# A second mixer's projections, norms, rotations and loads in another order

## The reference, cut to what matters

```python
hn = rms_norm(h, g_mix)
c_q, c_kv, k_r, q_d, k_d, v_d = split(hn @ w_in)      # 384, 256, 32, 512, 512, 512 columns
q  = rms_norm(c_q, g_cq) @ w_uq                       # 8 heads of 64 plain + 32 rotated features
kv = rms_norm(c_kv, g_ckv) @ w_ukv                    # 8 heads of 64 key + 64 value features
q_rope, k_rope = apply_rope(q[..., 64:]), apply_rope(k_r)        # k_rope is shared by the heads
o_mla = softmax((q_nope . k_nope + q_rope . k_rope) * scale) @ v_m
qd, kd = apply_rope(q_d), apply_rope(k_d)             # first 16 of 64 features of 8 heads
o_dil = dilated_attention(qd, kd, v_d)                # three masked patterns merged, as one mask
h = h + concat(rms_norm(o_mla), rms_norm(o_dil)) @ w_out
h = h + peer_ffn(...)                                 # product-key memory, then a gated embedding
```

## Time and profile before

| | |
|---|---|
| median of three runs | 2959.86 us (2959.3 to 2966.66) |
| profiled execution | 2961.28 us, span 2959.5 us, mean granted clock 0.967 |
| busy over the span | PE 2708.4 us (92%), DVE 1463.9 (49%), ACT 510.1 (17%), POOL 720.5 (24%) |
| second projection (to the end of its products) | 1341 to 1472 us |
| latent expansion | 1472 to 1544.7 us |
| attention's first scores | 1544.7 us |

### The profile page before, as it was taken

The page is one execution under the profiler, slowest core; times in us unless marked ns, Lnnn a source line. Parts: engine busy times, 40 slices in busy tenths (PEclk is TensorE's granted clock), DMA queues, the critical chain, the costliest instruction groups (busy, mean ns, idle before and its releaser), DMA issues. The chain is left out here.

```text
span 2959.5 us, 27511 instructions
## 1 busy us (share of the span) xinstructions
PE 2708.4 (92%) x10046; PEld 1524.1 (51%) x10046; DVE 1463.9 (49%) x3202; ACT 510.1 (17%) x1131; POOL 720.5 (24%) x588
## 2 busy tenths in 40 slices
PE   6999999999999689979989996999989889998888
PEld 3445634446444333324435565888879743333333
DVE  1045401203012322232137579889799986777773
ACT  2033300011001111221127420111122200000004
POOL 0000000000000011100000016655566565655640
PEclk9999999999999699999989998999999999999999
DMA  5101161210122899951210229999999699999983
GB/s 218 57 29 56 61 268 65 96 57 15 60 82 90 342 418 388 394 230 69 92 43 1 95 72 324 409 400 409 417 370 412 236 367 397 413 413 413 412 356 121
DMA packets 137559, 678.53 MB, mean 229 GB/s; under 512 B 20050, under 2 KB 21458, under 8 KB 105554
## 3 DMA queue, kind: packets, MB, share of 16 engines
q1 hardware_dynamic: 55986, 396.76, 33.5%
q0 software_dynamic: 80640, 276.88, 24.1%
q10 hardware_dynamic: 800, 3.15, 0.3%
HBM read 697.68 MB, written 33.55 MB: 247 GB/s over the span
## 5 line engine op out<-in xcount | busy, mean ns | idle before, releaser
L513 PE MATMUL ps<-hT,pm_coef_table 128*128 128x256 f32 (+1 forms) x2432 | 507.1, 371 | 30.4 <-DVE hT L439 24.4
L513 PEld LDWEIGHTS ps<-hT,pm_coef_table 128*128 128x128 f32 x2432 | 444.3, 192 | 87.2 <-issue 25.1
L2566 PE MATMUL ps<-hT 128*128 128x512 f32 x896 | 398.3, 598 | 41.6 <-DMA hT<-in_peer_v 28.2
L513 PE MATMUL ps<-hT,wring 128*128 128x512 f32 (+2 forms) x976 | 411.9, 583 | 10.5 <-PEq L694 2.9
L2415 POOL DMA_INDIRECT wring<-in_peer_u,pm_rows x256 | 336.0, 1313 | 300.8 <-DVE pm_coef L2676 159.3
L2415 POOL DMA_INDIRECT wring<-in_peer_v,pm_rows x256 | 325.0, 1269 | 235.0 <-DVE h_tok L2843 193.9
L2843 DVE SCALAR_TENSOR_TENSOR h_tok<-wring,pm_coef,h_tok 128x1024 f32<-128x1024 f32 x256 | 324.0, 1281 | 106.6 <-DMA wring<-in_peer_v,pm_rows 105.9
L2676 DVE CUSTOM_DVE_ANT_0 wring<-wring,pm_coef_table 128x1024 f32<-128x1024 f32 x256 | 303.2, 1218 | 35.0 <-DMA wring<-in_peer_u,pm_rows 34.4
L2566 PEld LDWEIGHTS ps<-hT 128*128 128x128 f32 x896 | 165.4, 190 | 274.3 <-issue 189.7
L513 PEld LDWEIGHTS ps<-hT,wring 128*128 128x128 f32 (+1 forms) x976 | 185.0, 191 | 231.6 <-issue 229.7
L1634 POOL DMA_INDIRECT hT<-xn_dram_out,row_token x24 | 24.5, 1020 | 1148.9 <-issue 1004.1
(11 more groups left out here) (423 smaller groups left out, 2829.5 us busy)
## 6 DMA issues: line engine op xcount, KB each, us to landing
ex_gu<-in_experts SPq DMA_DIRECT2D x32, 2048.0 KB, 19.3
pm_coef_table<-in_peer_uT SPq DMA_DIRECT2D x64, 1024.0 KB, 8.0
hT<-in_peer_v SPq DMA_DIRECT2D x64, 1024.0 KB, 8.0
ex_dn<-in_experts SPq DMA_DIRECT2D x47, 1024.0 KB
wring<-in_w_in SPq DMA_DIRECT2D x21, 2048.0 KB, 7.8
wring<-in_experts SPq DMA_DIRECT2D x15, 2048.0 KB
ada_w<-in_w_ada SPq DMA_DIRECT2D x12, 2048.0 KB, 12.1
g_dram_out<-pm_coef_table SPq DMA_DIRECT2D x56, 256.0 KB, 9.4
```

Of the source, the lines that this page charges most:

```text
L513: mm = env.nc.tensor.matmul(out, w[:, k, lo:hi], rhs(k), start=(k == 0), stop=(k == KD - 1))
L2566: mm = nc.tensor.matmul(env.ps[:, OUT[k], :], scores_at(i)[:, k // 2 * P:(k // 2 + 1) * P], vr[p % 2][:, i % 2 * D + k % 2 * WBLK:i % 2 * ...
```

## The change

1. In the projection the latents and the shared key part come before the values, with the list of weight blocks in the new order (0, 1, 3, 4, 2).
2. The squares, roots, inverses and scalings of the latents move from the expansion into the projection: on ScalarE behind the copy of the shared key part and ahead of the values' copies, on VectorE behind the rotation.
3. The four loads of the expansion are issued in the projection, ahead of the ring's loads. Their buffers are allocated around both stages.
4. In the expansion the transposed latents are copied out by VectorE (tiles 0, 2, 4) and ScalarE (tiles 1, 3). TensorE rotates the shared part first and waits only for the three query tiles before the queries' products and for the two others before the keys'. The heads' rotations stand ahead of the keys' products.
5. VectorE awaits the mask in front of the first step of kind 1.

```diff
@@ stage_second_project
-    blks = [env.take_block(t) for t in (q_t[-1], k_t[-1], v_t[-1], c_t[-1], kr_t)]
+    blks = [env.take_block(t) for t in (q_t[-1], k_t[-1], c_t[-1], kr_t, v_t[-1])]
 ...
             @block.sync
                 nc.sync.dma_start(perm[:], dram["perm_dil"]).then_inc(tab_in, 16)
+                nc.sync.dma_start(M.wq[:], dram["w_uq"]).then_inc(M.tab_in, 16)
+                nc.sync.dma_start(M.wkv[:], dram["w_ukv"]).then_inc(M.tab_in, 16)
+                nc.sync.dma_start(M.tab[0:QH], dram["rope_mla"]).then_inc(M.tab_in, 16)
+                nc.sync.dma_start(M.perm[0:QH, 0:QH], dram["perm_mla"]).then_inc(M.tab_in, 16)
                 load_blocks(env, sp)
 ...
             @block.scalar
                 nc.scalar.activation(M.kr[:], env.ps[0:QH, kr_t[0], :], ACT.Copy).then_inc(env.bank_free[kr_t[0]], 1)
+                for t in c_t + e_t:
+                    evacuated(env, act, t)
                 n = 0
                 for p, (lo, w) in enumerate(parts):
 ...
+                for i, t in enumerate(v_t):
+                    product_done(env, act, t)
+                    nc.scalar.activation(M.dv[:, i, :], env.ps[:, t[0], :], ACT.Copy).then_inc(env.bank_free[t[0]], 1)
 ...
             @block.vector
                 rope_dve(env, v, r_t, lambda j: M.dqk[:, j, :], tab, sn, cos_s, rope_s)
+                v.wait_ge(rms_s, 2)
+                nc.vector.reciprocal(ss[:], rs[:]).then_inc(inv_s, 1)
 ...
@@ stage_latent_expand
             @block.tensor
-                to_features(env, pe, c_t, lambda t, j: M.c[:, t, j * P:(j + 1) * P],
-                            lambda t, j: pe.wait_ge(nrm_s, (t + 1) + (NT if j >= CQ else 0)))
+                to_features(env, pe, c_t, lambda t, j: M.c[:, t, j * P:(j + 1) * P], lambda t, j: None)
                 pe.wait_ge(tab_in, 64)
-                for t in c_t:
+                rope_mm(env, pe, r_t[:1], perm[0:QH, 0:QH], roped, lambda j: None)
+                for t in c_t[:CQ]:
                     evacuated(env, pe, t)
 ...
+                rope_mm(env, pe, r_t[1:], perm[0:QH, 0:QH], lambda j: roped(j + 1), lambda j: evacuated(env, pe, q_t[j]))
+                for t in c_t[CQ:]:
+                    evacuated(env, pe, t)
 ...
-                rope_mm(env, pe, r_t, perm[0:QH, 0:QH], lambda j: M.q[:, j, :] if j < AH else M.kr[:],
-                        lambda j: evacuated(env, pe, q_t[j]) if j < AH else None)
@@ stage_attention
-                v.wait_ge(mask_in, 16)
                 for s in range(ns + 3):
                     if s < ns:
                         kind, hp, qt = steps[s]
+                        if kind == 1 and sem_of(s) == 0:
+                            v.wait_ge(mask_in, 16)
@@ program
-        stream(env, "w_in2", "w_out2", "w_ple_gate")
+        for b in (0, 1, 3, 4, 2):
+            env.blocks.append(dram["w_in2"][b])
+        stream(env, "w_out2", "w_ple_gate")
```

More of the change, by code:

```diff
@@ L1930, in stage_second_project @@
     q_t, k_t, r_t = env.tiles(4), env.tiles(4), env.tiles(8)
-    v_t, c_t = env.tiles(NT), env.tiles(NT)
+    c_t = env.tiles(NT)
     e_t, kr_t = env.tiles(NT), env.tile()
-    blks = [env.take_block(t) for t in (q_t[-1], k_t[-1], v_t[-1], c_t[-1], kr_t)]
+    v_t = env.tiles(NT)
+    blks = [env.take_block(t) for t in (q_t[-1], k_t[-1], c_t[-1], kr_t, v_t[-1])]
     tab_in, cos_s, rope_s = (env.sem("sp_" + n) for n in ("tab", "cos", "rope"))
+    sq_s, rms_s, inv_s, nrm_s = (env.sem("le_" + n) for n in ("sq", "rms", "inv", "nrm"))
+    parts = ((0, QR), (QR, KVR))
     with ExitStack() as st:
@@ L1951, in _ @@
                                          scale=DH ** -0.5 if j < 4 else 1.0).then_inc(env.bank_free[t[0]], 1)
[L1952 to L1955, removed]
+                for i, t in enumerate(c_t):
+                    product_done(env, act, t)
+                    nc.scalar.activation(M.c[:, i, 0:WBLK], env.ps[:, t[0], :], ACT.Copy).then_inc(env.bank_free[t[0]], 1)
                 for i, t in enumerate(e_t):
@@ L1985, in stage_latent_expand @@
[L1985 to L2012, removed]
@@ L2023, in _ @@
                     nc.scalar.activation(rs[:, p, :], ss[:, p, :], ACT.Sqrt, scale=1.0 / w, bias=env.eps[:, 0:1]).then_inc(rms_s, 1)
+                for i, t in enumerate(v_t):
+                    product_done(env, act, t)
+                    nc.scalar.activation(M.dv[:, i, :], env.ps[:, t[0], :], ACT.Copy).then_inc(env.bank_free[t[0]], 1)
+            @block.vector
+            def _(v):
+                v.wait_ge(tab_in, 32)
+                rope_dve(env, v, r_t, lambda j: M.dqk[:, j, :], tab, sn, cos_s, rope_s)
+                v.wait_ge(rms_s, 2)
+                nc.vector.reciprocal(ss[:], rs[:]).then_inc(inv_s, 1)
+                v.wait_ge(inv_s, 1)
+                for p, (lo, w) in enumerate(parts):
+                    for t in range(NT):
+                        x = M.c[:, t, lo:lo + w]
+                        nc.vector.tensor_scalar(x, x, ss[:, p, t:t + 1], None, ALU.mult).then_inc(nrm_s, 1)
@@ new lines, in _ @@
+            @block.tensor
+            def _(pe):
+                for b, tl in zip(blks[:2], (q_t, k_t)):
+                    w = block_view(env, pe, b)
+                    for j, t in enumerate(tl):
+                        project(env, pe, t, env.ps[:, t[0], :], w, j * P, (j + 1) * P, lambda k: env.hT[:, k, 0:S])
+                pe.wait_ge(tab_in, 32)
+                rope_mm(env, pe, r_t, perm[:], lambda j: M.dqk[:, j, :], lambda j: evacuated(env, pe, (q_t + k_t)[j]))
+                w = block_view(env, pe, blks[2])
+                for i, t in enumerate(c_t):
+                    by_token(env, pe, t, WBLK, w, i)
+                w = block_view(env, pe, blks[3])
+                for i, t in enumerate(e_t):
+                    by_token(env, pe, t, P, w, i)
+                project(env, pe, kr_t, env.ps[0:QH, kr_t[0], :], w, P, P + QH, lambda k: env.hT[:, k, 0:S])
+                w = block_view(env, pe, blks[4])
+                for i, t in enumerate(v_t):
+                    by_token(env, pe, t, WBLK, w, i)
@@ new lines, in stage_latent_expand, with _ @@
+def stage_latent_expand(env, M):
+    nc = env.nc
+    c_t = env.tiles(CQ + CKV)
+    r_t = env.tiles(1)
+    q_t = env.tiles(AH)
+    r_t += env.tiles(AH)
+    k_t = env.tiles(AH)
+    v_t = env.tiles(NT)
+    tab_in, cos_s, rope_s = M.tab_in, env.sem("le_cos"), env.sem("le_rope")
+    with ExitStack() as st:
+        T = lambda n, s: st.enter_context(nc.sbuf_tensor("le_" + n, s, F32))
+        sn, tab, perm, wq, wkv = T("sn", [P, 2, S]), M.tab, M.perm, M.wq, M.wkv
+        cT = T("cT", [P, CQ + CKV, S])
+        roped = lambda j: M.q[:, j - 1, :] if j else M.kr[:]
+        with nc.Block() as block:
+            @block.sync
+            def _(sp):
+                load_blocks(env, sp)
+            @block.scalar
+            def _(act):
+                for j in range(1, CQ + CKV, 2):
+                    product_done(env, act, c_t[j])
+                    nc.scalar.activation(cT[:, j, :], env.ps[:, c_t[j][0], :], ACT.Copy, scale=col(env, "g_cq", j)).then_inc(
+                        env.bank_free[c_t[j][0]], 1)
@@ L2036, in _ @@
             def _(v):
[L2037 to L2044, removed]
+                for j in range(0, CQ + CKV, 2):
+                    t = c_t[j]
                     product_done(env, v, t)
```

30 lines of the change are left out of this document (9 added, 21 removed).

## The result

The changed kernel took 2944.88 us (median of four, 2943.9 to 2949.93) beside 2962.73 us for the kernel before; ratio 0.9944, 95% interval 0.9926 to 0.9961. Its first profiled execution took 2949.93 us, its span is 2948.1 us, 11.4 us under the span before. The forecast was 2938, a gain of 22 on 2959.86, with a range of 2932.5 to 2945.5. Both medians lie in that range, the first one by 0.6 us; the profiled execution lies above it.

A forecast was written before the change was run, and what follows sets the result against it. TensorE plus its gaps, each with one late partner, was taken to bound the stretch; 5.0 + 2.5 + 3.9 + 1.5 + 6.1 + 3.2 = 22.2 us off the profiled 2961.28, 2938 against the median; range 2932.5 to 2945.5.

The forecast's parts named there:

- Steps a to f: In order: norms beside values, transposes, loads, queries' products, rotations ahead of keys, mask; gains sum to 22.2 us.
- d: Queries' products in the expansion: 20.9 us at the full clock instead of 22.40, gain 1.5 us, bounds 0 to 1.5.
- theory B: The change itself costs some 5 us elsewhere, above all because its loads are in flight at the projection's start.
- The first rival: TensorE's clock falls at the two short gaps, ahead of transposes and scores; 7.2 us lost, time 2945; chance 0.08.
- VectorE as the end of the expansion: VectorE still ends the expansion, so the rotations' gain of 6.1 us goes; time 2944; chance 0.04.
- the low clock through the expansion: Clock falls at the expansion's first boundary and stays low, 51 us more; all through, 2992; chance 0.02.
- Given back later: Attention's early start is lost behind it in a wait for an unmoved transfer; nearly all lost, 2957; chance 0.04.

The follow-up runs named there:

- clock_up: Changed kernel plus unused unit-matrix products on TensorE ahead of the transposes of the four token tiles just before the second projection; 2934.12 us, ratio 0.9904.
- loads_late: Changed kernel with the expansion's four loads moved back from the projection's start to the expansion's start; ratio 0.9964.
- again: Changed kernel without any edit, timed and profiled a second time; 2938.72 us (median of six), ratio 0.9919.
- loads_mid: Changed kernel with the expansion's four loads issued some 28 us into the projection instead of at its start; 2944.52 us, ratio 0.9937.
- mask_first: Changed kernel with the mask awaited at the head of attention again; attention 128.0 us, profiled span 2931.8 us.
- clock_up_before: Kernel before plus the same unused products ahead of the second projection, nothing else; ratio 1.0010.
- rot_late: Changed kernel with the eight heads' rotations behind the keys' products again, the shared part's rotation staying in front; ratio 0.9953.

## Why the prediction was right or wrong

Steps a to f came out almost to the tenth: 5.05 (forecast 5.0), 2.4 (2.5), 3.9 (3.9), 1.6 (1.5), 6.1 (6.1) and 3.2 (3.2) us. No new wait appeared, the values' block was in time, and VectorE ended 9.5 us ahead of the scores. With the projection at the full clock in both, the three stretches together go from 330.8 us (before) to 308.3 (clock_up), 22.5 us. That this meets 22.2 so closely is partly luck of the one profile: in the three other profiles with the old order the expansion took 68.1 to 68.3 us instead of 66.8, because the queries ran longer at the low clock or the loads came later.

Wrong was the step from the sum to the time. It said that "attention and everything behind it" moves forward whole, with PEclk 1.00 from 1341 us to attention, and that runs scatter "by a microsecond or more". In the profile after, the clock stood at 0.50 at the projection's start and once within attention, which took back 3.1 and 1.6 us of the 22.5, and the stretches outside the change took 6.6 us more (1.9 + 1.2 + 3.5); so some 11 us were left. These were terms that the sum had put at nothing.

In twelve profiles the projection's start alone moves from 1332.3 to 1347.3 us, and the last rows from 584.1 to 591.0, with kernels that do the same work there (two of them with unused products ahead of the projection); 20 runs of the kernel before lie between 2955.73 and 2971.58. In the profile of before the projection happened to start at the full clock; in eight of the ten profiles without added products it did not, and that takes up to 3.1 us. The range was worked out from the terms' bounds, which held but for 0.1 us in d, and left out this scatter, which is wider than any of them. The two series, 0.9944 and 0.9919, lie on both sides of the 0.9926 that I had forecast, and that the second median came within 1 us of 2938 is in part chance: the six times behind it spread over 17 us.

The traces show what most of this scatter is: time for which TensorE is busy at the low clock, in stretches that the change does not touch. A product takes about twice as long there (the shared part's rotation 2.02 us in loads_late, 1.02 in the changed kernel), so half of that time is lost. By this estimate, half of the last column of the table taken off the span, the four profiles after, again, clock_up and loads_mid lie between 2886.9 and 2889.0 us, though their spans lie between 2928.8 and 2949.6; the four with the old order lie between 2901.1 and 2907.5. The whole stretch ahead of the projection, in mask_first and in loads_mid, whose projections start 15.1 us apart (columns as in the earlier trace rows):

```profile
0.00:1332.30 1332.30, 1236.96 (x4227) 589.75 (x4227) 330.74 (x690) 235.27 (x512) 48.45 (x52) 0.97 0.41 163
0.00:1347.30 1347.30, 1248.87 (x4226) 598.91 (x4226) 331.02 (x690) 235.44 (x512) 48.45 (x52) 0.96 0.41 161
```

TensorE is busy 11.9 us longer for the same products; it is busy at 0.50 for 42.2 us in the one and 71.6 in the other, most of the difference before 230 us and between 940 and 1050 us. The last rows go with it too: 584.1 us with 9.1 us at the low clock (mask_first), 591.0 with 23.2 (clock_up_before). Executions without a profile show only their mean granted clock: 0.964 to 0.966 in the four of the first series of the changed kernel, 0.965 to 0.970 in the six of the second. By this estimate little is left for theory B, a cost of the change itself elsewhere. It is worked out from the traces; only at the projection's start has an edit (the added products) tested it.

The first rival (the clock falls at the two short gaps) is out, although its 2945 us is just what the first series measured: 1.00 behind 0.94 us at both boundaries, in the first profile after and again. Of short idle times that let the clock swing, which the Trainium skill tells of ("TensorE: Matmul & The Clock Gate", section "A second HAM failure mode: psum-queue depth-cycling"), the rows at these two boundaries show nothing. VectorE as the end of the expansion is out, so is the low clock through the expansion. "Given back later" is not shown: the last rows are longer in after and again (590.7 and 590.3), but shorter than before in clock_up and mask_first, which hold the same order of products, and longer in clock_up_before, which does not hold it.

That the terms add up was right only for the whole. Taken one at a time out of the changed kernel, the edits are worth 14.5 (loads), 8.9 (norms), 4.9 + 2.0 (rotations) and 4.2 us (mask), 34.5 together; the mask put alone into the old kernel is worth 1 at most. The loads' gap took over what the others gave (11.34 us instead of 3.88), and behind each of the four gaps the clock was low besides. The copies shared between VectorE and ScalarE and the shared part's rotation in front were not taken out alone.

Open: why the clock's level differs from run to run of one program, and what moves the rest of the last rows.

## What to carry to other kernels

Where one engine works through a chain with gaps, price the gaps together: one left in place can grow by what was saved ahead of it, as the loads' did, and can make the work behind it start at the low clock, as all four did here. Read the scatter of the untouched stretches, and TensorE's busy time at the low clock, from several profiles before putting a range on a small change; one profile gives the terms, not the total. Moving independent work (values) beside a short serial chain (norms) showed no cost here, nor did the loads one stage up, at either of the two places tried.

## What the runs showed of the hardware

The clock's level behind one and the same idle time differs from run to run. Behind 1.63 us (1.72 in rot_late) at the projection's start it stood at 0.50 for 2.8 to 6.2 us in eight of the ten profiles without added products, and at 1.00 from the start in two and in both with them. Behind 0.94 us and dense work it was always 1.00, behind 5.8 us or more always 0.50 at first. Behind 5.35 to 5.55 us of idle time 22 us into the program it was 1.00 at first in seven profiles, so the idle time just before does not settle the level. A low stretch can also stand within attention, where TensorE is at work most of the time (0.51 over 3.5 us in the profile after). Over a whole execution TensorE was busy at the low clock for 81.4 to 130.1 us, and the span goes with half of that.
